# Encoder layer in fp32: local queries and keys projected in turned form, four tiles of rows at a time

## The reference

```python
h = rmsnorm(x, g_pre_mix[l])
proj = h @ w_in[l]                       # (2048, 1024) @ (1024, 1536)
qa, ka, va, qb, kb, vb = jnp.split(proj, split_idx, axis=-1)   # 512, 128, 128, 512, 128, 128
...
out_a = global_axial_gqa(qa, ka, va, ...)   # per-head rmsnorm of qa, ka, then rotary, scores over all rows
out_b = window_sink_gqa(qb, kb, vb, ...)    # qb, kb as they are, scores over |i-j| <= 128
```

## Time and profile before

| | |
|---|---|
| median of 3 runs | 2723.7 us (2721.32 to 2725.67) |
| profiled execution | 2724.54 us, span 2722.7 us, mean granted clock 0.98 |
| TensorE, VectorE, ScalarE, POOL busy | 2599.4, 1908.2, 1395.2, 973.3 us |
| three-pass matmuls of the projection, 128x512 | 1152, of which each group of 384 is busy some 151 us |
| transposes 128x128 in the projection | 128 of xn, 160 of global heads, 160 of local heads |
| TensorE's wait for xn at the turn of x | 15.1 us in two waits |
| first instruction of the stage behind the projection | 349.87 us |

### The profile page before, as it was taken

One profiled execution on the slowest core, in us unless ns is written; L12 is line 12 of the kernel. 1 busy time (PEld: TensorE's weight loads), 2 busy tenths in 40 slices (PEclk: granted clock), 3 DMA queues, 4 the chain that ended last, 5 costly groups with the idle time before them and its releaser, 6 DMA issues. The chain is left out here.

```text
span 2722.7 us, 34573 instructions
## 1 busy us (share of the span) xinstructions
PE 2599.4 (95%) x11730; PEld 2099.2 (77%) x11730; DVE 1908.2 (70%) x2469; ACT 1395.2 (51%) x2082; POOL 973.3 (36%) x688
## 2 busy tenths in 40 slices
PE   7999969999999998989997999899999999999998
PEld 5888747777777776978776888778887888888886
DVE  5566569999999976875557877777785344456665
ACT  3333248888888886873344444444444333323431
POOL 1111159898899894430000333233232000000000
PEclk9999979999999998999998999999999999999999
DMA  5333242211222104634753544644455445445555
GB/s 175 108 102 107 83 114 61 48 42 40 68 53 49 32 13 134 181 92 144 213 176 122 164 144 160 228 135 155 144 173 185 153 158 197 143 142 199 202 180 198
DMA packets 290395, 355.09 MB, mean 130 GB/s; under 512 B 53971, under 2 KB 203603, under 8 KB 289212
## 3 DMA queue, kind: packets, MB, share of 16 engines
q1 hardware_dynamic: 271896, 340.05, 40.5%
q10 hardware_dynamic: 18340, 13.03, 1.7%
HBM read 225.65 MB, written 117.85 MB: 126 GB/s over the span
## 5 line engine op out<-in xcount | busy, mean ns | idle before, releaser
L697 POOL TENSOR_TENSOR p_sum<-p_sum,p_hi 128x1024 f32<-128x1024 f32 x160 | 383.5, 2397 | 31.8 <-issue 16.0
L109 PE MATMUL f_pr<-d_w,d_s 128*128 128x512 f32 x896 | 355.6, 397 | 6.8 <-DVE d_s L1943 4.5
L110 PE MATMUL f_pr<-d_w,d_s 128*128 128x512 f32 x896 | 355.0, 396 | 0.0
L111 PE MATMUL f_pr<-d_w,d_s 128*128 128x512 f32 x896 | 354.8, 396 | 0.0
L111 PE MATMUL f_pr<-wide,u_w_lo 128*128 128x512 f32 x896 | 351.0, 392 | 0.0
L776 DVE TENSOR_TENSOR p_lo<-s_ps,p_hi 128x1024 fp32r<-128x1024 f32 x256 | 313.4, 1224 | 39.6 <-ACT s_ps L730 35.2
L729 ACT ACTIVATE p_hi<-s_ps 128x1024 fp32r<-128x1024 f32 x256 | 263.7, 1030 | 127.5 <-PE s_ps L825 127.4
L762 DVE TENSOR_REDUCE part_max<-m_ps 128x1 f32<-128x1024 f32 x251 | 305.5, 1217 | 16.3 <-PE m_ps L807 16.0
L730 ACT ACTIVATE s_ps<-s_ps 128x1024 f32<-128x1024 f32 x256 | 262.1, 1024 | 0.0
L1980 POOL TENSOR_TENSOR d_rstd<-d_var,d_half 128x1 f32<-128x1 f32 x16 | 11.8, 739 | 614.4 <-DVE d_var L2045 614.4
L1936 ACT ACTIVATE d_s<-d_s 128x1024 fp32r<-128x1024 f32 x112 | 118.7, 1060 | 211.3 <-DMA d_s<-act_blocks 210.8
(11 more groups left out here) (239 smaller groups left out, 5911.3 us busy)
## 6 DMA issues: line engine op xcount, KB each, us to landing
d_s<-act_blocks SPq DMA_DIRECT2D x112, 512.0 KB, 4.0
act_blocks<-u_s_out SPq DMA_DIRECT2D x128, 256.0 KB, 6.4
act_blocks<-u_a_sum SPq DMA_DIRECT2D x96, 256.0 KB, 2.4
d_w_raw<-in_w_ffn_down SPq DMA_DIRECT2D x80, 256.0 KB, 3.9
u_w_first<-in_w_ffn_up SPq DMA_DIRECT2D x16, 1024.0 KB, 6.1
u_w_raw<-in_w_ffn_up SPq DMA_DIRECT2D x16, 1024.0 KB, 6.1
d_w_raw<-in_w_ffn_down SPq DMA_DIRECT2D x32, 512.0 KB, 4.6
x_in<-in_x SPq DMA_DIRECT2D x16, 512.0 KB, 4.4
```

Of the source, the lines that this page charges most:

```text
L109: nc.tensor.matmul(out, stat_hi, mov_hi, start=first, stop=False)
L110: nc.tensor.matmul(out, stat_hi, mov_lo, start=False, stop=False)
L111: return nc.tensor.matmul(out, stat_lo, mov_hi, start=False, stop=last)
L697: nc.gpsimd.tensor_tensor(p_sum[:, s], first, p_hi[:, (UNITS * n + u) % SLOTS].bitcast(F32), ALU.add).then_inc(added, 1)
```

## The change

The columns of w_in are put in another order in SBUF, so that global queries, keys and values and the local values come first (896 columns, `TURNED`), and the 640 of the local queries and keys last. Rows are now projected in two chunks, of 512 and 384 columns. The local queries and keys are projected in turned form: w_in is stationary (128 columns, two heads) and the turned x of four tiles (512 rows) moves, which makes five blocks (`local_block`) of 24 matmuls each for every four tiles, so that x's turned form is kept for four tiles. ScalarE copies a block's high part to SBUF, VectorE subtracts its low part, SP stores both in four pieces. The local splits, their turns and copies go. Blocks of a group follow chunk 1 of its third tile (t = 2, 6, 10); those of the last group follow all rows, between the last two turns of global heads. The turn of x of tile t+1 stands at the head of tile t. The split of the global values stands at the head of the work on the heads. The three banks of `pj` are handed out in turn. Loads: each slice of w_in comes in three pieces with a semaphore of its own, x of tile 1 behind slice 0, x of tile 2 ahead of the tables, x of tile 3 behind them. Chunk 0 of tile 1 is interleaved with the last four slices of tile 0. The loops are written out.

```diff
-        xt_hi = sb("xt_hi", [P, 2, KT, P], F32R)
-        xt_lo = sb("xt_lo", [P, 2, KT, P], F32R)
-        proj = sb("proj", [P, 2, IN_TOTAL])
-        qk_out = sb("qk_out", [P, 2, 10, 2 * HD])
-        qkb_out = sb("qkb_out", [P, 2, 10, 2 * HD])
-        qkb_t = sb("qkb_t", [P, 2, 10, P])
+        xt_hi = sb("xt_hi", [P, KT, GRP * P], F32R)
+        xt_lo = sb("xt_lo", [P, KT, GRP * P], F32R)
+        proj = sb("proj", [P, 2, TURNED])
+        outs = sb("qk_out", [P, 3 * IN_TOTAL])
...
+        bank_of, uses = {}, []
+        for g in range(NT // GRP):
+            rows = [(4 * g + i, c) for i in range(GRP) for c in range(2)]
+            blocks = [("block", BLOCKS * g + j) for j in range(BLOCKS)]
+            uses += rows[0:6] + blocks + rows[6:] if g < NT // GRP - 1 else rows + blocks
+        for i, use in enumerate(uses):
+            bank_of[use] = i % 3
...
+            def load_w(k):
+                if k >= 6:
+                    sp.wait_ge(w_lo_made, k - 5)
+                for to, of in ((slice(0, 768), slice(0, 768)), (slice(TURNED, IN_TOTAL), slice(768, 1408)), (slice(768, TURNED), slice(1408, IN_TOTAL))):
+                    sp.dma_start(arrive[k][:, to], w_tiles[k][:, of]).then_inc(w_loaded[k], 16)
...
+            load_w(0)
+            load_x(1)
+            for k in range(1, KT):
+                load_w(k)
+            load_x(2)
...
+            load_x(3)
...
+            def store_block(g, j):
+                n = BLOCKS * g + j
+                home, first, hi_rows, lo_rows = block_heads(j)
+                cols = slice(g * NB, (g + 1) * NB)
+                sp.wait_ge(local_lo_made, n + 1)
+                for i in range(2):
+                    half_rows = slice(i * HD, (i + 1) * HD)
+                    sp.dma_start(home[first + i, hi_rows, cols], local[half_rows, n % 2, 0]).then_inc(local_stored[n % 2], 16)
+                    sp.dma_start(home[first + i, lo_rows, cols], local[half_rows, n % 2, 1]).then_inc(local_stored[n % 2], 16)
...
+            for t in range(NT):
+                if 1 < t < NT - 2 and t % GRP != 3:
+                    load_x(t + 2)
+                if t >= 2:
+                    store_turned(t - 2)
+                if t % GRP == 2 and t < NT - GRP:
+                    load_x(t + 3)
+                    for j in range(BLOCKS):
+                        store_block(t // GRP, j)
+            store_block(NT // GRP - 1, 0)
+            store_turned(NT - 2)
+            for j in range(1, BLOCKS - 1):
+                store_block(NT // GRP - 1, j)
+            store_turned(NT - 1)
+            store_block(NT // GRP - 1, BLOCKS - 1)
...
+            def local_high(g, j):
+                n = BLOCKS * g + j
+                act.wait_ge(block_done, n + 1)
+                at_least(act, local_stored[n % 2], 64 * (n // 2))
+                nc.scalar.activation(local[:, n % 2, 0].bitcast(F32R), pj[:, bank_of["block", n]], ACT.Copy,
+                                     scale=SCALE if j < 4 else 1.0).then_inc(local_hi_made, 1)
...
+                act.wait_ge(w_loaded[k], 48)
                 nc.scalar.activation(w_hi[:, k], arrive[k], ACT.Copy).then_inc(w_hi_made, 1)
+                if k == 0:
+                    square(1)
                 if k == 2:
-                    square(1, 1, 0)
-            xt_high(1, 1)
-
-            def tile(t, s, p):
-                if not (isinstance(t, int) and t < 2):
-                    keep_turned(t - 2, s, p - 1, 0)
-                evacuate(t, s, p, 0)
-                if not known(t, NT - 2):
-                    square(t + 2, s, p + 1)
-                if not (isinstance(t, int) and t in (0, NT - 1)):
-                    xt_high(t + 1, 1 - s)
-                if not (isinstance(t, int) and t < 2):
-                    keep_turned(t - 2, s, p - 1, 1)
-                evacuate(t, s, p, 1)
-                evacuate(t, s, p, 2)
-                store_v(t, s)
-                if not (isinstance(t, int) and t == 0):
-                    store_qk(t - 1, 1 - s)
-
-            sweep(act, NT // 2, tile)
-            for t, b in ((NT - 2, 0), (NT - 2, 1), (NT - 1, 1)):
-                keep_turned(t, t % 2, NT // 2 - 1, b)
-            store_qk(NT - 1, 1)
-            keep_turned(NT - 1, 1, NT // 2 - 1, 0)
+                    xt_high(1)
+            for t in range(NT):
+                if 0 < t < NT - 1:
+                    xt_high(t + 1)
+                evacuate(t, 0)
+                if t > 0:
+                    store_global_v(t - 1)
+                if t < NT - 2:
+                    square(t + 2)
+                if t >= 2:
+                    keep_turned(t - 2)
+                evacuate(t, 1)
+                store_v(t)
+                if t % GRP == 2 and t < NT - GRP:
+                    for j in range(BLOCKS):
+                        local_high(t // GRP, j)
+            local_high(NT // GRP - 1, 0)
+            store_global_v(NT - 1)
+            keep_turned(NT - 2)
+            for j in range(1, BLOCKS - 1):
+                local_high(NT // GRP - 1, j)
+            keep_turned(NT - 1)
+            local_high(NT // GRP - 1, BLOCKS - 1)
...
+            def local_low(g, j):
+                n = BLOCKS * g + j
+                dve.wait_ge(local_hi_made, n + 1)
+                nc.vector.scalar_tensor_tensor(out=local[:, n % 2, 1], in0=pj[:, bank_of["block", n]], scalar=SCALE if j < 4 else 1.0,
+                                               in1=local[:, n % 2, 0], op0=ALU.mult, op1=ALU.subtract).then_inc(local_lo_made, 1)
+
+            def heads(t):
+                s = t % 2
                 nc.vector.drain()
-                dve.wait_ge(evacuated, 3 * t + 2)
+                dve.wait_ge(evacuated, 2 * t + 2)
+                at_least(dve, stored[s], 16 * (t // 2))
                 qk = heads_view(proj[:, s, 0:640], 10)
+                split(v_out[:, s, :, 0:HD], v_out[:, s, :, HD:], heads_view(proj[:, s, 640:768], NG)).then_inc(v_made, 1)
                 nc.vector.tensor_tensor(tmp[:], qk, qk, ALU.mult)
                 nc.vector.drain()
                 nc.vector.tensor_reduce(head_ss[:], tmp[:], AX, ALU.add)
                 nc.vector.drain()
                 nc.vector.tensor_scalar(head_var[:], head_ss[:], 1.0 / HD, EPS, ALU.mult, ALU.add).then_inc(head_var_made, 1)
-                if not known(t, NT - 2):
-                    normalise(t + 2, s)
-
-                dve.wait_ge(evacuated, 3 * t + 3)
-                at_least(dve, stored[s], 16 * p)
-                at_least(dve, qk_turned, 2 * t - 2)
-                split(qkb_out[:, s, 0:8, HD:], qkb_out[:, s, 0:8, 0:HD], heads_view(proj[:, s, 768:1280], 8))
-                split(qkb_out[:, s, 8:10, 0:HD], qkb_out[:, s, 8:10, HD:], heads_view(proj[:, s, 1280:1408], NG)).then_inc(local_done, 1)
-                split(v_out[:, s, :, 0:HD], v_out[:, s, :, HD:], heads_view(proj[:, s, 640:768], NG))
-
+                if t < NT - 2:
+                    normalise(t + 2)
...
+            variance(0)
+            dve.wait_ge(const_in, 32)
+            normalise(0)
+            xt_low(0)
+            for k in range(KT):
+                dve.wait_ge(w_hi_made, k + 1)
+                nc.vector.tensor_tensor(w_lo[:, k], arrive[k], w_hi[:, k].bitcast(F32), ALU.subtract).then_inc(w_lo_made, 1)
+                if k == 0:
+                    variance(1)
+                if k == 1:
+                    normalise(1)
+                if k == 3:
+                    xt_low(1)
+            for t in range(NT):
+                if 0 < t < NT - 1:
+                    xt_low(t + 1)
+                if t < NT - 2:
+                    variance(t + 2)
+                heads(t)
+                if t % GRP == 2 and t < NT - GRP:
+                    for j in range(BLOCKS):
+                        local_low(t // GRP, j)
+            for j in range(BLOCKS):
+                local_low(NT // GRP - 1, j)
...
+            def local_block(g, j):
+                n = BLOCKS * g + j
+                pe.wait_ge(xt_lo_made, GRP * (g + 1))
+                bank_free(("block", n))
+                cols = slice(TURNED + j * P, TURNED + (j + 1) * P)
+                for k in range(KT):
+                    last = three_passes(nc, pj[:, bank_of["block", n]], w_hi[:, k, cols], w_lo[:, k, cols], xt_hi[:, k], xt_lo[:, k],
...
-            def tile(t, s, p):
-                if isinstance(t, int) and t == 0:
-                    first_tile()
-                    return
-                chunk(t, s, 0)
-                if not known(t, NT - 1):
-                    turn(t + 1, 1 - s)
-                if not (isinstance(t, int) and t < 2):
-                    turn_qk(t - 2, s, 1)
-                chunk(t, s, 1)
-                chunk(t, s, 2)
-                turn_qk(t - 1, 1 - s, 0)
-
-            sweep(pe, NT // 2, tile)
...
+            turn(0)
+            pe.wait_ge(xt_lo_made, 1)
+            for k in range(KT):
+                pe.wait_ge(w_lo_made, k + 1)
+                for c in range(2):
```

(73 more changed lines are left out.)

180 lines of the change are left out of this document (78 added, 102 removed).

## The result

The changed kernel takes **2771.9 us** (median of 4 runs, 2768.4 to 2776.3) where the kernel before took 2724.7 in the same session (4 runs, 2721.3 to 2726.0): ratio 1.0177, 95% interval 1.0165 to 1.0189. Slower by 47 us; 2778 was predicted, with 2748 to 2792 as its range. The profiled execution took 2776.3 us (span 2774.5, mean granted clock 0.969; the granted clock is TensorE's, as a share of its full speed); it is the highest of the four.

The account below looks back on a forecast made before the run. TensorE's instruction stream was taken as the bound, with the new order adding bare waits for xn. Head, stream, waits, clock and tail: 11.2 - 7.9 + 40.1 + 21.6 - 11.0 = +54.0 us, forecast 2778 us, range 2748 to 2792.

Parts of the forecast that it names:

- The nine waits: TensorE at nine turns of x in the stream, waiting for xn: 4.45 us of stream each, 40.1 us added.
- The clock behind them: TensorE's lowered clock after each of the nine waits: 2.4 us each, 21.6 us added.
- The stream: TensorE's work over tiles 4 to 15, without the local turn: 7.9 us shorter.
- The head: Start of the projection to tile 3's end: 11.2 us longer, uncertain by 6, with a 7.5 us wait for xn.
- The tail: Last matmul to the next stage: 5.9 us where 16.9 stood, 11.0 us less.
- the turns do not wait: Rival at the turns of x: xn is ready, so waits and their clock loss go; 2706 us, chance 0.07.
- More waits than I count: Rival on block stores and buffer reuse, or a head 10 us longer: 2790 to 2800 us, chance 0.10.

Follow-up runs that it names:

- run with the turn late: Changed kernel with the turn of x of tile t+1, and ScalarE's copy of it, put back behind chunk 0 of tile t: 2728.3 us.
- run that kept TensorE busy: Changed kernel with 19 unused matmuls of 512 columns ahead of each of the nine turns that wait: 2751.5 us.
- run with the split late: Changed kernel with only the split of the global values moved behind the normalised x on VectorE: 2764.6 us.
- run with the last blocks early: Changed kernel with the last group's five blocks put behind chunk 1 of tile 14, so tile 15's heads end the projection: 2783.6 us.
- turn late with the low part inside: Changed kernel with x's turn behind chunk 0, values' split behind xn, and the turned x's low part inside the ropes' step in some tiles: 2707.4 us.
- best run: Changed kernel with late turn and split, low part inside ropes' step, tile 1's head work later, two gain loads for ten: 2702.4 us.
- run with the head's order: Changed kernel with tile 1's turned-x copy and low part behind the sixth weight slice, TensorE mixing tile 1 in from the seventh: 2771.3 us.

## Why the prediction was right

The direction and the mechanism held at each place where the working named one, and the sum came out 6 us too high. All terms but the tail's erred to the same side, so that the range was not met by errors that cancel. Term by term, by the changed kernel's trace:

- **The nine waits** were put at 4.3 us each from the chain of durations; they are 4.30 to 4.32, behind the tiles that were named. In stream time they were put at 4.45 each, 40.1 us; the trace shows 38.8 us of idleness. The run with the turn late shows cause and not only company: without this order 43.6 us go.
- **The clock behind them** was the term that was mis-sized: 2.4 us each, 21.6; the stretches give 2.0 each, 18.2, and the run that kept TensorE busy 17.6 in the stream. The single losses run from 1.4 to 3.0 us, those of the earlier trace rows from 1.7 to 3.0; I had four rows and took their mean: behind the waits of 6.93, 4.96, 3.94 and 3.07 us the stretches of the earlier trace rows give 8 x (1 - clock) = 2.6, 2.2, 1.7 and 3.0 us. That every long wait of the stream costs clock was borne out: the nine of 4.3 us were followed by 0.62 to 0.83 over 8 us, the nine of 3.8 to 4.2 in the run with the split late by 0.64 to 0.83. Short ones mostly cost none: seven of the eight of 1.3 to 1.9 us in the run with the turn late were followed by 1.00, the eighth, of 1.92 us, by 0.79.
- **The stream** was put 7.9 us shorter. From the end of tile 3 to the last matmul's end are 281.1 us (110.6 to 391.7) where 232.5 were; less 38.8 of waits and 18.2 of clock, 8.4 us shorter. This term and the waits share a border: the 4.45 us counted in the end of the last matmul, 0.15 us a wait, which the 38.8 leave to the stream.
- **The head**: +11.2 was put, +10.1 came (110.6 against 100.5). The wait ahead of the turn of tile 3 was put at 7.5 us and is 6.2. Its chain was right: slice 3 waits for ScalarE, and VectorE's 11.7 us of heads (41.14 to 52.86) decide xn of tile 3. That x of tile 2 is not late once it stands ahead of the tables was right too; put behind them again it costs 4 to 6 us, which my expectation of that run missed. What I did not name is how near the gains' loads stand behind that chain: with the slices in order a gain's landing takes its place.
- **The tail**: 5.9 us from the last matmul to the hand-over was put, 6.06 came (391.69 to 397.75), where 16.9 were. The run with the last blocks early gives this part alone, 11.7 us.

Sum at the hand-over: 10.1 + 48.6 - 10.8 = 47.9 us, against 54.0; of the 6.1 us between, the clock has 3.4, the waits 1.3, the head 1.1, the stream 0.5, and the tail takes 0.2 back.

Of the rivals, "the turns do not wait" is what the kernel becomes once its order is mended: 2706 us was worked out for it, 2707.4 measured for the turn late with the low part inside. The parts agree as well: in that run's trace the stream is 225.2 us long, 223.3 without its 1.9 of waits, where 224.6 was put and 232.5 stood. So the turned form of the projection saves what its matmul and transpose counts say; but the order of the queues cost 64.5 us (2771.9 against 2707.4), most of it by the place of one turn (43.6). "More waits than I count" did not come: from 60 to 400 us TensorE has no wait but the nine.

Open: which part of the 14 us that the stream gained between the two runs with a late turn belongs to the split and which to the low part's place; what makes the queue slow behind the ten gains; and whether the best run's order would help the kernel before as well, which was not tried.

## What to carry to other kernels

When work is taken out of an in-order queue, look at what it was covering: write down, for each wait on that queue, what now lies between the instruction that starts the chain and the one that needs its end, and sum the chain's durations. If nothing lies between, every step of the chain is paid at each turn of the loop (here 4.3 us, nine times), and TensorE's clock on top (here 2 us for each wait of about 4); moving one instruction behind the next independent block can win most of it back (here 43.6 of 47 us). Then find which engine's queue ends last in the new order before moving anything in the head, since a mended order can simply hand the wait to a load (here 7.8 us for the last gain).

## What the runs showed of the hardware

- The streams' waits of 3.8 to 4.3 us on TensorE, nine in the changed kernel and nine with the split late, were followed, 18 times in 18, by 8 us at a mean clock of 0.62 to 0.83, of which the first 2 us were at 0.50 to 0.76; those of 1.3 to 1.9 us in the run with the turn late once in eight. The same wait of 4.3 us cost between 1.4 and 3.0 us of work. Which of the nine cost much is not chance: in the run with the head's order, which has the same nine, their clocks are 0.65, 0.79, 0.80, 0.70, 0.79, 0.61, 0.82, 0.63 and 0.79, in the changed kernel 0.68, 0.79, 0.82, 0.72, 0.79, 0.62, 0.83, 0.64 and 0.79. What decides it no run shows.
- A wait of about 2 us went either way: the one of 2.12 us ahead of the turn of tile 2 was followed by a clock of 0.79 over 8 us in the changed kernel (at 44.88 us), and by 1.00 in the run with the turn late (at 43.92).
- Matmuls that write nothing of use were worth their place here, where TensorE would have idled anyway: with 171 of them the stream was 17.6 us shorter, the kernel 20.3 by the medians.
- Ten broadcast loads of 32 KB in pieces of 256 bytes (64 floats to each of 128 partitions) stood in front of slice 6 of the weights, and ScalarE then waited 12.85 us for it, with the DMA engines busy for 0.15 of the time from 20 to 32 us. They moved 43 GB/s there, and 391 from 10 to 16 us with the weights in the queue; what holds the loads while those engines are mostly idle no run shows. Two such loads in their place landed 5.0 and 3.9 us after issue.
- What one load's order is worth depends on what stands in front of it: the gains' landing cost nothing in the changed kernel and 7.8 us with the slices in order.
